# A two-layer decoder trunk on one core: norm sums of the heads by matmuls with ones, weights' low parts moved from GpSimd to VectorE, and a reordered start

## Chip, cores and metric

The kernel runs on one core of a Trainium2 chip. The metric is the device time of one execution in microseconds (us), median of the runs. The engines are TensorE (PE; its weight loads are listed as PEld), VectorE (DVE), ScalarE (ACT), GpSimd (POOL) and SyncE (SP), which issues most of the DMAs.

## What is computed

The input x has 512 tokens and 1024 features in float32. Layer 0 adds a causal pooling mixer and an MLP; then keys and values are projected once; layer 1 adds a differential attention of 8 heads over them and another MLP. The reference, cut:

```python
def _rmsnorm(x, g):
    y = x * lax.rsqrt(jnp.mean(x * x, axis=-1, keepdims=True) + EPS)
    return y * g

def _mlp(h, w_in, w_out):                 # 1024 -> 4096 -> 1024
    return jnp.square(jax.nn.relu(h @ w_in)) @ w_out

# layer 0: window means over 2, 4, 8, 16 tokens, one window for each of 4 groups of 256 features
m = pooled - hg                           # hg: _rmsnorm(x, norm_mix[0]) by groups
x = x + einsum('bsgc,gcd->bsgd', m, pool_w) * pool_scale
x = x + _mlp(_rmsnorm(x, norm_mlp[0]), w_mlp_in[0], w_mlp_out[0])
kv = _rmsnorm(x, kv_norm) @ w_kv
k = _rmsnorm(kv[..., :1024].reshape(b, s, 8, 2, 64), k_norm)
v = kv[..., 1024:].reshape(b, s, 8, 128)
# layer 1, for each head with its two key and query halves c
q = _rmsnorm((h @ w_q).reshape(b, s, 8, 2, 64), q_norm) * 64 ** -0.5
p = softmax(q_c @ k_c.T + bias[distance], causal)
o = (p[:, :, 0] - lam * p[:, :, 1]) @ v
x = x + _rmsnorm(o, subln) * (1 - lambda_init) @ w_o
x = x + _mlp(_rmsnorm(x, norm_mlp[1]), w_mlp_in[1], w_mlp_out[1])
```

## The kernel before

Features lie on the 128 partitions and tokens along the free axis (`xT`, 8 chunks of 128 x 512). Each large product is made of three matmuls (`product`, L1373): every operand is split into a high part (fp32r, rounded by ACT) and a low part (the rest, made by a subtraction), and high x high, high x low and low x high are summed in a PSUM bank. There are eight banks, `O[0:4]` and `I[0:4]`. Weights come through two raw buffers of 128 x 2048; ACT writes `w_high`, DVE `w_low` (`split_low`, L914). A unit counter runs through them: `w_high`, `w_low` and `w_used` count units split and used. Each engine has its own stream of instructions, written out by hand, and semaphores tie them together; the order in a stream is the order of execution.

**Start** (before L1542). x is loaded by token, its squares are summed on ACT (L719), and three tiles of 128 tokens are scaled on DVE (L1129) and one on ACT (L728), while PE turns x into `xT`. Then PE mixes: for each of 8 chunks one matmul by zeros over the whole bank (L1516), which opens the sum, and four matmuls of tokens with the bands (L1519). ACT and DVE split the result. After all eight mixes and a small bias product (L1526) come the 48 matmuls with the pooling weights (L1530), and then MLP 0. One weight unit in this stretch is split on Pool.

**MLPs** (`mlp`, L1469). Input units of 256 columns, then per quarter seven products of a Strassen-like scheme. The change doesn't touch them.

**Heads.** Unit `U_HEAD + 2n` holds the K and Q weights of head n (2 x 1024 columns of buffer 1), the next unit the V weights (buffer 0). During head h PE makes the scores of h and then projects K, Q, V of head n = h + 1 (`head`, L1633). K and Q must be normed over 64 features, which lie on partitions. So ACT copies the projection out of PSUM (`kf`, `qf`), PE turns it (`turn`, L1561: four transposes of 128 x 128), ACT squares what it turned (`square_raw`, L772), DVE reduces over 64 columns (`kq_reduce`, L1173) and adds eps, ACT takes the root, DVE inverts it and spreads it over the columns of `ksq` and `qsq` (`kq_inverses`, L1193), PE turns these back, and DVE multiplies (`kq_norms`). The output O of a head is normed the same way one head later (`of`, `o_squares`, `o_sums`, `o_inverses`, `o_norm`). The order on PE in a head is: scores of tiles 0 and 1, turns of V and O, scores of tiles 2 and 3, projection of K (24 matmuls), of Q (24), turn of the probabilities (10 transposes), turns of K and Q as projected, 18 matmuls of V's projection, turns of the spread K, Q and O norms, 6 matmuls of V, and probabilities by values. In head 0 there is no projection of K, as it is made earlier. The low parts of the K and Q weights are made on Pool in two halves (`split_low_halves`, L540), and DVE passes the news on (`pass_low`, L921). Heads 1 to 6 are one loop. Between MLP 0 and head 0 lies a passage: K, Q and V of head 0, the statistics of the norm before K and V (`norm_stats`, L1382, four matmuls of 128 x 128 with two columns of ones), and K of head 1. The last head is written apart and runs beside the output projection (`wo_part`).

## Time and profile before

| | us |
|---|---|
| median of 3 runs | 969.94 (968.29 to 970.57) |
| the profiled execution | 970.49 |
| its span on the core | 968.7 |

| engine | busy us | share | instructions |
|---|---|---|---|
| PE | 954.0 | 98% | 5143 |
| PEld | 813.1 | 84% | 5143 |
| DVE | 681.1 | 70% | 959 |
| ACT | 464.6 | 48% | 588 |
| POOL | 82.3 | 8% | 66 |

The chain of work that ended last is PE's for 85% of the span, DVE's for 7%, ACT's for 4%. Matmuls overlap with the next ones, so their durations don't add up; the distance from one start to the next does. A number behind `x` in the rows counts records. In brackets or behind the last bar stands the engine's idle time and what ended it.

### The profile page before, as it was taken

To read this page: it belongs to the slowest core of one execution; us is meant where nothing else is said; L and a number is where in the kernel's file an instruction comes from. 1 tells how busy PE (TensorE), PEld (TensorE's weight loads), DVE (VectorE), ACT (ScalarE), POOL (GpSimd) and SP (SyncE) were. 2 spreads that over 40 slices of the span, in tenths; PEclk is the share of its full clock that TensorE was granted. 3 is DMA by queue.
4 is the path that set the end of the run, shared out by engine and by line. 5 is a ranking of instruction groups with operands and counts; after the bars stand their busy time and mean duration, and the time that the engine had idled before them with its cause. 6 is when DMAs were issued, how large, how long until landed. Compare 5 with 4: busy or idle time off the path is not lost.

```text
span 968.7 us, 13034 instructions
## 1 busy us (share of the span) xinstructions
PE 954.0 (98%) x5143; PEld 813.1 (84%) x5143; DVE 681.1 (70%) x959; ACT 464.6 (48%) x588; POOL 82.3 (8%) x66
## 2 busy tenths in 40 slices
PE   8999999999999999999999999999999999999998
PEld 7788998998898898778888887888888888888877
DVE  4976766666676678877777777667767676677685
ACT  7644334334333437576666765345433433433432
POOL 1201000000000000122222220000000000010010
PEclk9999999999999999999999999999999999999999
DMA  6427682385457534143232222334676269238534
GB/s 228 138 84 232 131 260 87 88 228 163 118 113 205 160 59 130 44 115 86 72 86 84 78 74 93 109 102 113 191 200 191 90 125 261 89 87 225 165 98 120
DMA packets 99212, 128.94 MB, mean 133 GB/s; under 512 B 3201, under 2 KB 61618, under 8 KB 99162
## 3 DMA queue, kind: packets, MB, share of 16 engines
q1 hardware_dynamic: 85178, 98.33, 30.8%
q0 software_dynamic: 13984, 29.91, 16.8%
q8 instruction: 35, 0.57, 0.2%
q14 instruction: 15, 0.12, 0.0%
HBM read 126.11 MB, written 4.74 MB: 135 GB/s over the span
## 4 chain that ended last, share of the span: by engine, by line
PE 85%; DVE 7%; ACT 4%; issue 3%; DMA 1%; SPq 0%; DVEq 0%; ACTq 0%
PE bank L1375 27%; PE bank L1377 26%; PE bank L1376 26%; PE bank L1565 2%; DVE w_low L918 2%; PE bank L1575 2%; DVE kq_sum_buf L1175 1%; ACT w_high L655 1%; PE bank L1519 1%; DMA work<-in_x_dram 1%; ACT h_high_buf L613 1%; ACT w_high L607 0%; DVE work L1273 0%; ACT a_high_buf L812 0%; DVE a_low_buf L1244 0%
## 5 line engine op out<-in xcount | busy, mean ns | idle before, releaser
L1375 PE MATMUL bank<-h_high_buf,w_high 128*128 128x512 f32 x640 | 252.5, 394 | 0.7 <-DVE h_low_buf L927 0.4
L1377 PE MATMUL bank<-h_high_buf,w_low 128*128 128x512 f32 x640 | 249.4, 390 | 0.0
L1376 PE MATMUL bank<-h_low_buf,w_high 128*128 128x512 f32 x640 | 249.2, 389 | 0.0
L918 DVE TENSOR_TENSOR w_low<-raw,w_high 128x2048 fp32r<-128x2048 f32 (+1 forms) x68 | 147.3, 2166 | 66.8 <-ACT w_high L655 49.1
L1375 PE MATMUL bank<-a_high_buf,w_high 128*128 128x256 f32 (+1 forms) x592 | 184.4, 312 | 2.2 <-DVE a_low_buf L927 1.4
L1377 PE MATMUL bank<-a_high_buf,w_low 128*128 128x256 f32 (+1 forms) x592 | 183.0, 309 | 0.0
L1376 PE MATMUL bank<-a_low_buf,w_high 128*128 128x256 f32 (+1 forms) x592 | 182.8, 309 | 0.0
L1375 PEld LDWEIGHTS bank<-h_high_buf,w_high 128*128 128x128 f32 x640 | 120.2, 188 | 28.7 <-issue 2.2
L1377 PEld LDWEIGHTS bank<-h_high_buf,w_low 128*128 128x128 f32 x640 | 120.1, 188 | 25.4
L1376 PEld LDWEIGHTS bank<-h_low_buf,w_high 128*128 128x128 f32 x640 | 120.3, 188 | 23.6
L664 ACT ACTIVATE work<-work 128x512 f32<-128x512 f32 x64 | 40.1, 632 | 181.3 <-DVE work L971 181.2
L655 ACT ACTIVATE w_high<-raw 128x2048 fp32r<-128x2048 f32 x40 | 76.5, 1912 | 94.2 <-PE bank L1377 90.9
L1375 PEld LDWEIGHTS bank<-a_high_buf,w_high 128*128 128x128 f32 x592 | 113.0, 191 | 10.0 <-issue 2.3
L1377 PEld LDWEIGHTS bank<-a_high_buf,w_low 128*128 128x128 f32 x592 | 113.0, 191 | 5.8
L1376 PEld LDWEIGHTS bank<-a_low_buf,w_high 128*128 128x128 f32 x592 | 113.1, 191 | 5.4
L971 DVE SCALAR_TENSOR_TENSOR work<-bank,rstd_bc 128x512 f32<-128x512 f32 x64 | 43.5, 687 | 70.9 <-PE bank L1377 70.7
L1375 PE MATMUL bank<-w_high,a_high_buf 128*128 128x512 f32 x224 | 87.7, 392 | 1.5 <-DVE w_low L918 1.1
L1376 PE MATMUL bank<-w_low,a_high_buf 128*128 128x512 f32 x224 | 87.2, 389 | 0.0
L1377 PE MATMUL bank<-w_high,a_low_buf 128*128 128x512 f32 x224 | 87.2, 389 | 0.0
L987 DVE TENSOR_TENSOR a_low_buf<-work,a_high_buf 128x1792 fp32r<-128x1792 f32 (+2 forms) x34 | 64.9, 1909 | 6.1 <-ACT a_high_buf L671 6.1
L594 ACT ACTIVATE w_high<-raw 128x2048 fp32r<-128x2048 f32 (+1 forms) x29 | 48.5, 1673 | 33.1 <-PE bank L1377 33.1
L671 ACT ACTIVATE a_high_buf<-work 128x1792 fp32r<-128x1792 f32 (+2 forms) x34 | 54.5, 1602 | 7.4 <-DVE work L982 7.4
(152 smaller groups left out, 1171.1 us busy)
## 6 DMA issues: line engine op xcount, KB each, us to landing
raw<-in_w_mlp_out_dram SPq DMA_DIRECT2D x24, 1024.0 KB, 6.2
raw<-in_w_mlp_out_dram POOLq DMA_DIRECT2D x24, 1024.0 KB, 8.7
raw<-in_w_mlp_in_dram SPq DMA_DIRECT2D x16, 1024.0 KB, 5.5
work<-in_w_mlp_out_dram SPq DMA_DIRECT2D x8, 1024.0 KB, 4.7
work<-in_w_mlp_in_dram SPq DMA_DIRECT2D x8, 1024.0 KB, 6.7
raw<-in_w_kv_dram SPq DMA_DIRECT2D x16, 512.0 KB, 4.0
xT<-in_w_mlp_out_dram SPq DMA_DIRECT2D x8, 1024.0 KB, 4.7
xT<-in_w_mlp_in_dram SPq DMA_DIRECT2D x8, 1024.0 KB, 7.0
```

Of the source, the lines that this page charges most:

```text
L594: act.activation(w_high_buf[s][:, 0:cols], src[:, 0:cols], ACT.Copy).then_inc(w_high, 1)
L655: act.activation(w_high_buf[u % 2][:, :], mlp_raw[l][OUT_RAW[p]], ACT.Copy).then_inc(w_high, 1)
L664: act.activation(b[:, 0:8:7, :] if j == 0 else b[:, A12:A22 + 1, :], relu_buf[j].rearrange("p (h n) -> p h n", h=2), ACT.Square)\
L671: act.activation(operand(a_high_flat, n, first, last), pre[n % 2][:, first:last, :].rearrange("p s n -> p (s n)"), ACT.Copy)\
L918: dve.tensor_tensor(w_low_buf[s][:, 0:cols], src[:, 0:cols], f32(w_high_buf[s][:, 0:cols]), ALU.subtract)\
L971: dve.scalar_tensor_tensor(relu_buf[j], I[2 * (n % 2) + j][:, :], 0.0, rstd_bc, ALU.max, ALU.mult).then_inc(z_taken, 1)
L987: dve.tensor_tensor(operand(a_low_flat, n, first, last), pre[n % 2][:, first:last, :].rearrange("p s n -> p (s n)"), f32(operand(a_high_fl ...
L1375: pe.matmul(acc, w_hi, m_hi, start=start, stop=False, skip_group_check=onto)
L1376: pe.matmul(acc, w_hi, m_lo, start=False, stop=False, skip_group_check=onto)
L1377: return pe.matmul(acc, w_lo, m_hi, start=False, stop=stop, skip_group_check=onto)
L1565: last = pe.transpose(b[:, i * P:(i + 1) * P], src[:, i * P:(i + 1) * P], ident[:, :])
L1575: done = pe.matmul(O[b + c][:, 0:n], w[r, q], m[r, 0:n], start=first, stop=last)
```

## The change

For the heads:

- The squares of K, Q and O are taken on ACT from the bank of the projection itself. PE sums them over the partitions by four matmuls of 128 x 128 with two columns (`column_sums`), with `half_ones` (one for each half of 64 partitions) for K and Q, and with `all_ones` for O. The turns of K, Q and O as projected go, and so do the three reduces on DVE.
- K and Q are handled apart, each with semaphores of its own: K's sum stands in the middle of Q's projection, the turn of K's spread norm behind it, ahead of the turn of the probabilities.
- Pool subtracts nothing in the heads. DVE makes the low parts of the K and Q weights, the Q half behind the scores of tiles 0 and 1 (`kq_weights_rest`), the K half behind `k_low` (`kq_weights_first`).
- Head 6 is written out, as `head(H - 2, ..., last=True)`, and splits two parts of the output projection's input, which now lie at chunks 10 and 15.

For the start and the passage: the roots of all token tiles are taken together, tile 3 is squared on DVE, the bands are loaded behind the parameters, the matmuls by zeros go, the pooling weights are split in two halves, all on ACT and DVE, and the pooling products stand between the mixes. The dot products for lambda move behind the pooling. In the passage V's weights are split earlier, and the projections are interleaved in another order.

The diff, cut:

```diff
+        half_ones = sb("half_ones", [P, 2])
...
-            sp.dma_start(band_sb, bands).then_inc(bands_landed, 16)
...
+            sp.dma_start(band_sb, bands).then_inc(bands_landed, 16)
...
-                split_low_halves(h, POOL_UNITS[1 + h])
...
-            for i in range(TT):
+            for i in range(TT - 1):
                 act.wait_ge(x_landed[i], 16)
                 act.activation(h_tok[:, i, :], x_tok[:, i, :], ACT.Square, accum_out=tok_ss[:, i:i + 1]).then_inc(tok_sq, 1)
...
+            act.wait_ge(tok_last_sq, 1)
+            act.activation(tok_root[:, :], tok_ss[:, :], ACT.Sqrt, scale=1.0 / D, bias=eps[:, 0:1]).then_inc(tok_rooted, 1)
...
+            act.activation(w_high_buf[0][:, 0:UNIT // 2], raw[0][:, 0:UNIT // 2], ACT.Copy).then_inc(pool_half_high, 1)
...
+            def head(h, first, last=False):
+                n = h + 1
                 exps(h)
+                bring_table(ACT.Sqrt)
                 if not first:
-                    o_squares(h - 1, I[3])
-                copy_k(h + 1)
-                split_v(h + 1)
-                bring_table(ACT.Sqrt)
-                copy_q(h + 1)
-                split_high_first(U_HEAD + 4 + 2 * h, kq_landed(h + 2))
-                at_highs(h)
-                project(h + 1)
-                kq_roots(h + 1)
+                    square_k(n)
+                    copy_k(n)
+                split_v(n)
+                if last:
+                    o_high(0)
+                    o_high(1)
+                k_root(n)
+                split_high_first(n + 1, kq_landed(n + 1))
+                square_q(n)
+                copy_q(n)
+                k_high(n)
+                at_highs(h, range(1))
+                q_root(n)
                 if not first:
-                    o_roots(h - 1)
+                    o_roots(h - 1, I[3])
+                at_highs(h, range(1, 3))
                 bring_table(ACT.Exp)
-                kq_highs(h + 1)
-                split_high_rest()
+                q_high(n)
+                split_high_rest(U_HEAD + 2 + 2 * n)
                 o_copies(h, I[3])
+                o_squares(h, I[3])
...
+            dve.wait_ge(x_landed[TT - 1], 16)
+            dve.tensor_tensor_reduce(out=h_tok[:, TT - 1, :], in0=x_tok[:, TT - 1, :], in1=x_tok[:, TT - 1, :], scale=1.0, scalar=0.0,
+                                     op0=ALU.mult, op1=ALU.add, accum_out=tok_ss[:, TT - 1:TT]).then_inc(tok_last_sq, 1)
...
                 scores(h, 0)
                 scores(h, 1)
-                pass_low(h + 1)
+                kq_weights_rest(n)
                 combine(h, 0)
                 v_lows(h)
...
                 combine(h, 3)
-                split_low(U_HEAD + 3 + 2 * h, 0, 1024)
-                if not first:
-                    o_sums(h - 1)
-                at_lows(h)
-                kq_sums(h + 1)
-                kq_inverses(h + 1)
+                split_low(U_HEAD + 1 + 2 * n, 0, 1024)
+                if last:
+                    o_low(0)
+                    o_low(1)
+                add_k_eps(n, I[0])
+                k_inverses(n)
+                k_norm(n, I[0])
+                add_q_eps(n, I[1])
+                at_lows(h, range(1))
+                q_inverses(n)
                 if not first:
                     o_inverses(h - 1)
-                kq_norms(h + 1)
+                at_lows(h, range(1, 3))
+                k_low(n)
+                kq_weights_first(n + 1)
+                q_norm(n, I[1])
                 if not first:
                     o_norm(h - 1, O[3])
-                kq_lows(h + 1)
-                take_v(h + 1)
+                q_low(n)
+                take_v(n)
...
-                pe.matmul(I[c % 4][:, :], a_high_buf[:, 0, 0:P], a_high_buf[:, 0, :], start=True, stop=False)
...
+            for c in range(4):
+                mix(c)
+            pe.wait_ge(pool_half_low, 1)
+            pe.wait_ge(xt_copied, len(ACT_CHUNKS))
+            pool_group(0)
+            mix(4)
+            mix(5)
...
+            pool_group(1, lambda: pe.wait_ge(bias_rows_ready, 2))
+            mix(6)
+            mix(7)
+            pe.wait_ge(w_low, 1)
+            pool_group(2)
+            pool_group(3)
             mlp(0)
...
+            def column_sums(b, src, ones):
+                for i in range(TT):
+                    last = pe.matmul(b[:, 2 * i:2 * i + 2], src[:, i * P:(i + 1) * P], ones[:, :], start=True, stop=True)
+                return last
...
-                    turn(of, I[3], o_copied, h - 1, o_raw_turned)
+                    o_sums(h - 1, I[3])
...
-                project(None, 1, 1024, I[1], a_high_buf, a_low_buf, w_used)
+                project(None, 1, 1024, I[1], a_high_buf, a_low_buf, None, range(0, 4))
+                k_sums(n, I[0])
+                project(None, 1, 1024, I[1], a_high_buf, a_low_buf, w_used, range(4, KC))
+                turn(ksq, I[0], k_spread, n, k_turned)
                 turn_probs(h)
-                turn_raw(n)
+                q_sums(n, I[1])
                 pe.wait_ge(w_low, U_HEAD + 2 + 2 * n)
                 pe.wait_ge(v_low, n)
-                project(None, 0, 0, I[2], h_high_buf, h_low_buf, None, range(0, 6))
-                turn(ksq, I[0], k_spread, n, k_turned)
+                project(None, 0, 0, I[2], h_high_buf, h_low_buf, None, range(0, 5))
                 turn(qsq, I[1], q_spread, n, q_turned)
                 if not first:
                     turn(osq, O[3], o_spread, h - 1, o_turned)
-                project(None, 0, 0, I[2], h_high_buf, h_low_buf, w_used, range(6, KC))
+                project(None, 0, 0, I[2], h_high_buf, h_low_buf, w_used, range(5, KC))
```

## Rows read from the trace of the kernel before

**Rows 1.** The page: busy us, share of the span and instructions of each engine.

```profile
PE 954.0 (98%) x5143; PEld 813.1 (84%) x5143; DVE 681.1 (70%) x959; ACT 464.6 (48%) x588; POOL 82.3 (8%) x66
```

**Rows 2.** Stretches: length, then busy us by engine, PEclk, DMA share, GB/s.

```profile
0.00:24.90 24.90, 21.25 (x115) 18.06 (x116) 12.08 (x16) 18.67 (x30) 3.55 (x10) 0.93 0.70 232
...
374.64:402.65 28.01, 26.54 (x126) 20.42 (x124) 23.00 (x35) 18.82 (x31) 0.87 (x1) 1.00 0.20 57
402.65:424.43 21.78, 19.50 (x116) 15.64 (x116) 18.23 (x51) 15.72 (x34) 5.61 (x5) 1.00 0.35 100
424.43:577.44 153.01, 152.43 (x878) 126.07 (x877) 111.03 (x318) 103.33 (x222) 35.21 (x24) 1.00 0.30 86
```

**Rows 3.** Timeline of PE in head 2: start, us, engine, line, form, count.

```profile
450.82 1.09 PE L1565 MATMUL bank<-ident,work 128*128 128x128 f32 x8
...
465.39 1.04 PE L1565 MATMUL bank<-ident,work 128*128 128x128 f32 x8
...
470.63 1.54 PE L1565 MATMUL bank<-ident,work 128*128 128x128 f32 x12
```

**Rows 4.** Waits of PE's weight loads: us in total, times, longest.

```profile
PEld bank L1565 <- DVE work L1198: 4.2, 7, 1.1
```

**Rows 5.** Timeline of PE in MLP 0, around a norm sum and a turn.

```profile
50.15 0.95 PE L1390 MATMUL bank<-all_ones,work 128*128 128x2 f32 x8
50.96 0.49 PE L1375 MATMUL bank<-h_high_buf,w_high 128*128 128x512 f32 x1
51.28 0.40 PE L1376 MATMUL bank<-h_low_buf,w_high 128*128 128x512 f32 x1
...
54.51 0.60 PE L1396 MATMUL bank<-ident,work 128*128 128x128 f32 x4
54.86 0.48 PE L1375 MATMUL bank<-h_high_buf,w_high 128*128 128x512 f32 x1
```

**Rows 6.** Groups by line: count, busy us, mean ns, idle time before.

```profile
L1390 PE MATMUL bank<-all_ones,work 128*128 128x2 f32 x24 | 2.9, 245 | 0.4 <-DVE work L1273 0.4
```

**Rows 7.** Timelines of POOL, ACT and DVE in head 2.

```profile
448.99 2.38 POOL L548 TENSOR_TENSOR w_low<-raw,w_high 128x1024 fp32r<-128x1024 f32 x1 [5.96 <-ACT w_high L610]
...
459.55 1.05 ACT L594 ACTIVATE w_high<-raw 128x1024 fp32r<-128x1024 f32 x1
460.62 1.28 ACT L797 ACT_TABLE_LOAD   x1
...
460.63 1.23 DVE L918 TENSOR_TENSOR w_low<-raw,w_high 128x1024 fp32r<-128x1024 f32 x1 [1.08 <-ACT w_high L594]
```

**Rows 8.** Timeline of DVE in head 0.

```profile
404.11 0.28 DVE L1227 CUSTOM_DVE_ANT_0 work<-bank,work 128x128 f32<-128x128 f32 x1
...
412.86 1.22 DVE L918 TENSOR_TENSOR w_low<-raw,w_high 128x1024 fp32r<-128x1024 f32 x1
```

**Rows 9.** Timelines of ACT, DVE, PE and POOL at the start.

```profile
10.89 1.15 ACT L728 ACTIVATE work<-work,tok_rstd 128x1024 f32<-128x1024 f32 x1
...
12.04 2.05 ACT L732 ACTIVATE xT<-bank 128x512 f32<-128x512 f32 x4
...
14.79 0.75 DVE L927 SCALAR_TENSOR_TENSOR a_low_buf<-bank,params,a_high_buf 128x512 fp32r<-128x512 f32 x1 [1.49 <-ACT a_high_buf L613]
...
17.49 0.47 PE L1516 MATMUL bank<-a_high_buf 128*128 128x512 f32 x1
...
22.70 4.58 POOL L537 TENSOR_TENSOR w_low<-raw,w_high 128x2048 fp32r<-128x2048 f32 x1 [20.45 <-ACT w_high L594]
22.78 4.59 DVE L1143 CUSTOM_DVE_ANT_0 work<-work 128x64 f32<-128x64 f32 x1
...
36.25 0.39 PE L1375 MATMUL bank<-h_high_buf,w_high 128*128 128x512 f32 x1
```

**Rows 10.** A short stretch at the start, columns as in rows 2, and a DMA issue.

```profile
14.00:15.00 1.00, 1.00 (x6) 1.00 (x5) 0.21 (x1) 0.66 (x2) 0.00 (x0) 0.50 1.11 355
...
work<-in_bands_dram SPq DMA_DIRECT2D x1, 572.0 KB, 7.9
```

More of the change, by code:

```diff
@@ L531, in _ @@
             done(pool.memset(all_ones[:, :], 1.0))
+            done(pool.memset(half_ones[:, :], 0.0))
+            done(pool.memset(half_ones[0:HD, 0:1], 1.0))
+            done(pool.memset(half_ones[HD:P, 1:2], 1.0))
             pool.memset(eps[:, :], EPS).then_inc(consts_ready, 1)
@@ new lines, in _ @@
+            act.wait_ge(params_ready, 1)
+            mix_high(0)
+            mix_high(1)
+            copy_xt(0)
+            act.activation(w_high_buf[0][:, UNIT // 2:], raw[0][:, UNIT // 2:], ACT.Copy).then_inc(w_high, 1)
+            mix_high(2)
+            mix_high(3)
+            split_in(0, 0)
+            mix_high(4)
+            mix_high(5)
+            act.wait_ge(bias_done, 1)
+            act.activation(bias_rows[0:H, 0:S], O[3][0:H, :], ACT.Copy).then_inc(bias_rows_ready, 1)
+            mix_high(6)
@@ L843, in _ @@
-            square_raw(0, 1, qsq)
             norm_root_step(NORM_KV)
-            kq_roots(0)
+            k_root(0)
+            q_root(0)
             bring_table(ACT.Exp)
-            kq_highs(0)
-            split_high_rest()
-            def head(h, first):
+            act.wait_ge(lam_dot, 2)
+            act.activation(lam_exps[:, :], lam_dots[:, :], ACT.Exp).then_inc(lam_exp, 1)
+            k_high(0)
+            q_high(0)
+            split_high_rest(U_HEAD + 2)
+            square_k(1)
@@ new lines, in _ @@
+            mix_low(1)
+            dve.wait_ge(w_high, 1)
+            dve.tensor_tensor(w_low_buf[0][:, UNIT // 2:], raw[0][:, UNIT // 2:], f32(w_high_buf[0][:, UNIT // 2:]), ALU.subtract)\
+               .then_inc(w_low, 1)
+            mix_low(2)
+            mix_low(3)
+            dve.wait_ge(xt_copied, len(ACT_CHUNKS))
+            add_pooled(0)
+            add_pooled(1)
+            mix_low(4)
+            mix_low(5)
+            add_pooled(2)
+            add_pooled(3)
+            mix_low(6)
@@ L1284, in _, with head @@
             dve.wait_ge(kq_eps_ready, 1)
[L1285 to L1288 removed]
+            add_k_eps(0, O[0])
+            add_q_eps(0, O[1])
             norm_invert(NORM_KV)
+            k_inverses(0)
+            q_inverses(0)
             norm_keep(NORM_KV, I[3])
+            k_norm(0, O[0])
+            q_norm(0, O[1])
             take_v(0)
+            k_low(0)
+            q_low(0)
+            dve.wait_ge(lam_exp, 1)
+            dve.tensor_scalar(neg_lam[:, :], lam_exps[:, 1:2], lam_exps[:, 0:1], -LAMBDA_INIT, ALU.subtract, ALU.add).then_inc(lam_ready, 1)
             dve.wait_ge(lam_ready, 1)
[L1294 removed]
+            def head(h, first, last=False):
+                n = h + 1
                 dve.wait_ge(t_landed, 16 * h + 16)
@@ new lines, in _ @@
+            for c in range(4):
+                mix(c)
[4 more added lines that the diff above has]
+            mix(5)
+            pe.wait_ge(bias_in_landed, 32)
+            pe.wait_ge(x_ready, X_POOL)
+            pe.matmul(O[3][0:H, :], rel_sb[:, :], bucket_sb[0:NB, :], start=True, stop=True).then_inc(bias_done, 1)
+            pool_group(1, lambda: pe.wait_ge(bias_rows_ready, 2))
+            mix(6)
```

412 lines of the change are left out of this document (212 added, 200 removed).

## Prediction

> **What bounds the kernel now.** I read the page's busy shares first: the matmul engine (PE) is busy in 98% of the span, VectorE (DVE) 70%, ScalarE (ACT) 48% and GpSimd (Pool) 8% [rows 1]. A busy PE is not yet PE at its peak, so the second view is the table of stretches, which I cut where the code changes stage [rows 2]. It shows PE busy for 152.4 of 153.0 us in heads 1 to 6 (25.50 us a head). Only three stretches leave it idle: the start (3.7 of 24.9 us), the passage from MLP 0 to the first head (1.5 of 28.0), and head 0 (2.3 of 21.8). The third view is the timeline of PE alone, where distances from start to start give the true price of an instruction, since ends overlap. In the steady head the only wait worth a name is that of the twelve turns at 470.63 for the spread K norms [rows 3], 4.2 us over seven heads as the waits view has it, in part hidden by the pipeline [rows 4]. So in the heads an instruction taken off DVE or Pool gains nothing, and each put on PE costs its full time.
>
> **Turns replaced by sums (24 times).** Before, the norm of K, Q and O of each head goes: a turn (4 transposes on PE), a square on ACT, a reduce on DVE. After, ACT squares the projection as it is, and PE sums over its partitions by 4 matmuls with ones, 2 columns wide. PE loses one turn and gains one sum, for each of K, Q, O in 8 heads. The kernel already does both things elsewhere. A turn starts at 54.51 and the product after it at 54.86: 0.35 us. A sum of the same form (128x128 stationary f32, 2 columns moving) starts at 50.15 and the next product at 50.96: 0.81 us; its row says x8, two records for each of the 4 matmuls [rows 5], and the groups by line have 24 records for 12 such matmuls [rows 6], while the two turns at 450.82 are x8, one record for each transpose [rows 3]. A swap therefore costs 0.81 - 0.35 = 0.46 us of PE. Among other turns I take the same difference: 4 records of 0.11 more. 24 swaps are 11.0 us, if PE has no slack to put them in.
> The Trainium skill's page "TensorE: Matmul & The Clock Gate" (section Back-to-back issue gap) gives matmuls of 1 to 64 columns a floor near 25 ns. By that rule, an estimate from this page, a sum would take 0.1 us and each swap would gain 0.25. The trace disagrees: 0.81 us for such a sum [rows 5]. The rule is a rival below.
>
> **The steady head.** Before, a head has a chain of 18 transposes (10 of L1601 for the probabilities, then L1565 x8 at 465.39), one of 12 (470.63) and one of 8 inside the scores (450.82) [rows 3]. After: scores hold turn V and the O sum (+0.46); K's sum stands alone inside the Q projection (+0.81, and 0.09 for one more break in the run of products, as 0.32 against 0.23 shows behind a sum [rows 5]); the turn of the spread K, the turn of the probabilities and the Q sum follow each other (14 turns and 8 sum records against 18 turns, +0.46); then turns of Q and O (8 instead of 12, -0.45). That is +1.37. The wait for the spread norms goes, since K's are now made during the Q projection: -0.31. I sum 25.50 + 1.06 = 26.56 us.
> Is that cover real? I laid ACT and DVE against it, from the start of the head's scores. DVE takes over the low parts of the K and Q weights, twice 1024 columns. DVE's own row for 1024 columns is 1.23 us, next to 2.38 on Pool [rows 7]: +2.3 us in all, and its three reduces go. The first half stands behind the first scores, on DVE's queue in front of combine and the later scores; it ends at +2.9, PE wants it at +3.8. DVE ends its last combine at 0.6 + 8.75 [rows 8] + 1.15 = +10.5. ACT ends its exponentials near +8.8, then come a table load (1.3), square and copy of K (0.5 each) and V's high part (1.05) until +12.3 [rows 7], and V's low part on DVE until +13.5. K's root, inverse and spread end at +14.5, while PE comes to the turn at +15.8: 1.3 us to spare. The Q sum needs the copy of Q at +17.0, PE is there at +17.3. The normed O of the head before must be ready at +24.7, and is at +24.4, as the other half of the weights (1.15) stands before it. ACT's square of O ends at +1.2, PE wants it at +1.3. Four margins, two of them thin. Covered, they cost nothing; uncovered, about 0.5 us a head. Heads 1 to 6: 6 x 1.06 = +6.4. Head 6 also has two O parts split on DVE and ACT ahead of K's sum: +0.4.
>
> **Head 0** has no K projection (it is made earlier), so it lacks those 5.5 us of cover. DVE's chain from the first scores (404.11) to V's low part (412.86) takes 8.75 [rows 8] without a break, and ACT's exponentials end before its last combine does. After, with scores at 403.4 and 1.15 more in it, the last combine ends at 413.3; ACT brings the square-root table (1.3) and splits V (1.05) until 414.1; DVE's low part ends at 415.25 and K's spread at 416.3. PE, done with the Q projection and K's sum at 412.2, now has the turn of the spread K ahead of the probabilities and waits about 4.2 us, where before it waited 2.3 in the whole head. Walked on, scores of head 1 start at 426.7 against 424.43 [rows 2].
>
> **Passage to the first head.** Two sums (+0.9), a wait of 1.0 for V's low weights and 0.7 for the inputs of the Q projection are new; the waits for kv sums, for the turned norm and for V mostly go, as V is scaled earlier. My walk gives scores of head 0 at 402.8 against 402.65, so +0.15, between -1.5 and +1.5 (the idle time there is 1.5 [rows 2]). With head 0: +2.3.
>
> **Last head and output projection.** One more sum (+0.46) inside the scores; but the probabilities' end no longer waits for the reduce of O on DVE: -0.85. Net -0.4.
>
> **The start.** The 8 matmuls by zeros go (each lies 0.31 ahead of what follows it, as the one at 17.49 does [rows 9]: 2.5 us), and pooling products move between the mixes. All tokens' roots are now taken together: the first scaling on DVE comes at 10.8 instead of 9.4. ACT scales tile 3 (1.15) and copies a bank before it copies the parameters, so the first mix goes from 12.3 to about 13.2. Then ACT has three bank copies (2.05 for 4) and half the pool weights (1.0) until 15.6, DVE its half (1.15) and two low parts (0.75 each, 0.66 from start to start) until 18.1 [rows 9]. From there PE has all its work: 48 products of 0.228 (10.95), 4 mixes of 0.87, the bias matmul 0.95 and breaks 0.2 make 15.6, so MLP 0 starts at 33.8 instead of 36.25 [rows 9]: -2.45. The granted clock fell to 0.50 from 14 to 15 us, the lower of its levels (1.2 GHz), after PE had waited for the parameters from about 10.9 to 12.3 [rows 10]; the same may come at another place, hence +-2. The bands are issued behind seven small parameter loads on SP's queue; they are 572 KB, took 7.9 us from issue among the loads of x [rows 10], and PE needs them only at 13.2, later than before; the loads ahead of them are 25 KB, so this is covered.
> The first custom instruction of DVE is an open price. It took 4.59 us for 64 columns at 22.78, beside a Pool subtraction from 22.70 of 4.58 [rows 9]. Both end together, so I hold it for blocked by Pool, and the new one (the square of tile 3) then costs about 1.2 at 9.0, when Pool does nothing. The Trainium skill, page "SBUF — State Buffer", section "SBUF: two separate sides", says the same: DVE with two SBUF inputs and GpSimd exclude each other for a whole instruction.
>
> **The sum** against the profiled execution, 970.49 us around a span of 968.7: -2.45 + 2.3 + 6.4 + 0.4 - 0.4 = +6.2, so 976.7. On the median of the runs, 969.94, it gives 976.1. The MLPs have the same code.
>
> **Rivals.** (1) Other side: a narrow sum is cheaper than a turn among other work. Place: the 24 sums; price: if its 8 records hid under running products down to 0.1 us, each swap would gain 0.25 instead of costing 0.46: 969.94 + 6.2 - 24 x 0.71 = 959.1. The kernel is faster than before once a swap comes out 0.26 us cheaper than I have it. For it: 2 columns instead of 128. Against it: [rows 5], measured between such products. Chance 7%. (2) The first custom instruction is slow of itself: DVE, ACT and PE start 3.5 to 4 us later; 980. For it: the first custom instruction of the program was the one of 4.59 [rows 9]. 10%. (3) DVE or ACT becomes late in each head, at one of the thin margins: 0.5 us x 7 = 3.5, 979.6. 13%. (4) The change doesn't bring head 0 and the passage the waits that I see: -4, 972.1. 10%. My forecast, 976.1 with 974 to 978 around it: 60%.
>
> **Range and chances.** 971.5 to 981 holds cases 2, 3, 4 and the forecast, with the clock's +-2 on the start; outside lies case 1 and some of a sum of 2 and 3. A measurement of this kernel can tell 0.2% (1.9 us) from no change. Faster 0.07 (case 1), within 0.06 (the low end of case 4), slower 0.87.
>
> **What would show it.** In the profile after: sums x8 with 0.8 us to the next product; steady heads of 26.5 us; PE waiting about 4 us at the first turn of K in head 0; MLP 0 starting near 33.8; the first custom instruction near 9 us lasting 1.2. A head shorter than 25.5 would break the first step, one above 27 the cover.

## The result and the profile after

The changed kernel takes 981.14 us, the median of its runs (980.11 to 983.11), beside 969.95 (968.29 to 970.57) for the kernel before: a ratio of 1.0119, interval 1.0103 to 1.0134, so 1.2% slower. The forecast was 976.1 with a range of 971.5 to 981.0. The direction was right; the time lies 5 us above the forecast and just above the range. The profiled execution is the 983.11 one, with a span of 981.3.

The page after, its rows of busy time and of PE's clock in 40 slices of 24.5 us:

```profile
PE 965.2 (98%) x5231; PEld 828.6 (84%) x5231; DVE 682.7 (70%) x961; ACT 461.4 (47%) x592; POOL 46.5 (5%) x54
...
PEclk8999999999999999989999999999999999999999
```

PE has 88 more records and 11.2 us more busy time than in [rows 1]; Pool has lost 36 us and DVE gained only 1.6, as the three reduces per head are gone. The new thing is in the PEclk row: an 8 in the first slice and an 8 in the eighteenth (417 to 441.6 us), behind the wait in head 0. The stretches of the code's stages say what each digit is worth. Columns as in [rows 2]: length, busy time by engine, PEclk, DMA share, GB/s; the stretches are the start until the first pooling product, the pooling, the passage, head 0, and heads 1 to 6.

```profile
0.00:20.46 20.46, 15.28 (x73) 13.56 (x74) 8.57 (x14) 12.79 (x21) 1.65 (x12) 0.83 0.72 245
20.46:36.44 15.98, 15.98 (x86) 13.08 (x84) 11.77 (x18) 8.77 (x13) 6.92 (x5) 1.00 0.46 129
374.98:403.34 28.36, 27.16 (x135) 21.38 (x134) 22.98 (x38) 20.13 (x35) 0.00 (x0) 1.00 0.20 56
403.34:431.63 28.29, 24.33 (x125) 20.28 (x124) 18.19 (x50) 16.11 (x35) 1.15 (x2) 0.82 0.29 77
431.63:590.60 158.97, 158.83 (x951) 135.50 (x950) 116.77 (x320) 104.50 (x230) 5.89 (x11) 1.00 0.29 83
```

Beside [rows 2] that gives a ledger. It is made from span to span (968.70 and 981.32), from one PE start to the next, and its lines add up to the difference of 12.62. In the last column the side after is taken from a run in which TensorE's clock stayed at 2.4 GHz in that stretch (the start from the one below with K's norm first, head 0 from the one with idle products); the side before is its profile as it is.

| stretch | before | after | change | forecast | at full clock |
|---|---|---|---|---|---|
| start to MLP 0 | 36.25 | 36.44 | +0.19 | -2.45 | -2.26 |
| MLP 0 to the passage | 338.39 | 338.54 | +0.15 | 0 | +0.15 |
| passage | 28.01 | 28.36 | +0.35 | +0.15 | +0.35 |
| head 0 | 21.78 | 28.29 | +6.51 | +2.15 | +2.31 |
| heads 1 to 6 | 153.01 | 158.97 | +5.96 | +6.8 | +5.96 |
| last head to the end | 391.27 | 390.72 | -0.55 | -0.4 | -0.55 |
| sum | 968.70 | 981.32 | +12.6 | +6.2 | +6.0 |

The start needs care, because the kernel before has a low clock there too, around the row of [rows 10]:

```profile
13.00:14.00 1.00, 1.00 (x9) 0.91 (x8) 0.30 (x1) 1.00 (x4) 0.00 (x0) 0.78 1.10 360
...
15.00:16.00 1.00, 1.00 (x6) 1.00 (x6) 0.54 (x1) 0.00 (x0) 0.00 (x0) 0.50 0.96 209
16.00:17.00 1.00, 1.00 (x6) 0.90 (x5) 0.20 (x1) 0.92 (x2) 0.00 (x0) 0.51 0.18 40
```

It is low from about 13.6 to 17.0 us, with PE busy all the time. In the two larger groups of runs of the kernel before, those with a mean clock of 0.998, as in its profile, have a median of 970.2, those with 1.0 one of 968.7. So an estimate of its start at full clock is 36.25 - 1.5 = 34.8. The changed start ends at 33.99 and 34.47 in the two profiles that have a whole clock there. Clock against equal clock the new order then brings 0.3 to 0.8 us and not 2.26, and the change as a whole costs 7.4 to 7.9 us and not 6.0. Where both sides have the clock low for 3.4 us the new order brings 1.2 to 1.5 (four profiles, 34.73 to 35.09).

**The heads.** The timeline of PE in head 1 of the kernel after (start, duration, line, form, records) answers to [rows 3]:

```profile
443.59 0.95 PE L1655 MATMUL bank<-half_ones,work 128*128 128x2 f32 x8
444.40 0.49 PE L1456 MATMUL bank<-a_high_buf,w_high 128*128 128x512 f32 x1
...
447.27 0.60 PE L1680 MATMUL bank<-ident,work 128*128 128x128 f32 x4
447.70 1.25 PE L1716 MATMUL bank<-ident,work 128*128 128x128 f32 x10
448.80 0.95 PE L1655 MATMUL bank<-half_ones,work 128*128 128x2 f32 x8
```

A sum has its 8 records and 0.81 us until the next product. Almost no idle time stands in these heads: 158.83 busy us in 158.97. So the steady head (1 to 5), 26.44 us, is the price of PE's instructions and nothing else. Head 6, with the two O parts, is 26.75.

**The start.** Timeline of PE, with idle time and its releaser in brackets, then the one custom instruction of DVE at the start, then the clock in short stretches:

```profile
9.38 1.09 PE L1581 MATMUL bank<-ident,work 128*128 128x128 f32 x8 [0.26 <-DMA work<-in_x_dram]
13.07 0.31 PE L1585 MATMUL bank<-ident,work 51*128 51x51 f32 x1 [2.60 <-ACT xT L732]
13.73 6.51 PE L1603 MATMUL bank<-work 128*128 128x143 f32 x28 [0.35 <-ACT params L743]
```

```profile
9.36 1.22 DVE L1171 CUSTOM_DVE_ANT_0 work<-work 128x1024 f32<-128x1024 f32 x1 [8.36 <-DMA work<-in_x_dram]
```

```profile
12.00:13.00 1.00, 0.00 (x0) 0.00 (x0) 1.00 (x2) 0.93 (x2) 0.00 (x0) 0.95 1.01 320
13.00:14.00 1.00, 0.58 (x2) 0.48 (x3) 1.00 (x3) 0.58 (x2) 0.00 (x0) 0.50 0.94 301
14.00:16.00 2.00, 2.00 (x10) 2.00 (x10) 1.11 (x2) 2.00 (x4) 0.00 (x0) 0.50 1.06 341
...
19.00:20.00 1.00, 1.00 (x7) 1.00 (x7) 0.32 (x2) 1.00 (x3) 0.00 (x0) 0.64 0.00 0
```

PE idles for 2.6 us before the turn of the parameters, the clock drops to its lower level (1.2 GHz) at the end of that, and the mixes then run on it: 28 matmuls of 143 columns take 6.5 us. The custom instruction takes 1.22 us for 1024 columns, not the 4.59 for 64 of [rows 9].

**Head 0.** PE's row at the turn of the spread K, and the clock around it:

```profile
417.02 1.11 PE L1680 MATMUL bank<-ident,work 128*128 128x128 f32 x4 [3.79 <-DVE work L1253]
```

```profile
413.00:417.00 4.00, 0.23 (x2) 0.00 (x0) 2.87 (x6) 2.62 (x5) 0.00 (x0) 0.83 0.49 135
417.00:419.00 2.00, 1.98 (x10) 1.98 (x11) 0.69 (x1) 1.29 (x4) 0.00 (x0) 0.50 0.83 237
...
423.00:425.00 2.00, 2.00 (x6) 1.56 (x5) 2.00 (x5) 1.47 (x2) 0.00 (x0) 0.50 0.00 0
425.00:426.00 1.00, 1.00 (x4) 0.76 (x4) 0.80 (x1) 0.00 (x0) 0.00 (x0) 0.55 0.00 0
```

The wait that was forecast (4.2 us) is there, 3.79 us for the spread norm made at L1253. What follows it is not in the forecast: from 417 to about 425.9 PE is busy at half clock. 8.9 us at half speed do what 4.45 would do at full speed. The run with idle products below has 4.2. The Trainium skill, page "TensorE: Matmul & The Clock Gate", section Terms, prices the penalty as the time below full clock times the share of pulses left out. By it, as an estimate, the whole low stretch, from about 415.7 to 425.9, would cost 5.1 us; that is more than the 4.2, as PE was idle until 417.0.

### The profile page after: what moved, and what is told of

Read it like the earlier page. It is cut to its first block, busy times and chain, and to the rows that moved or that the text cites. A ratio compares the mean times of both kernels' runs of the same rounds, so it can differ in the third digit from the quotient of the medians.

```text
span 981.3 us, 13176 instructions
## 1 busy us (share of the span) xinstructions
PE 965.2 (98%) x5231; PEld 828.6 (84%) x5231; DVE 682.7 (70%) x961; ACT 461.4 (47%) x592; POOL 46.5 (5%) x54
## 4 chain that ended last, share of the span: by engine, by line
PE 89%; DVE 5%; ACT 3%; issue 2%; DMA 1%; SPq 0%; DVEq 0%; ACTq 0%
PE bank L1456 28%; PE bank L1458 27%; PE bank L1457 27%; DVE w_low L952 2%; PE bank L1655 2%; PE bank L1680 2%; PE bank L1690 2%; PE bank L1603 1%; PE bank L1716 1%; ACT w_high L663 1%; DMA work<-in_x_dram 1%; ACT work L773 0%; ACT w_high L600 0%; ACT a_high_buf L621 0%; DVE work L1017 0%
## 5 line engine op out<-in xcount | busy, mean ns | idle before, releaser
L952 DVE TENSOR_TENSOR w_low<-raw,w_high 128x2048 fp32r<-128x2048 f32 (+1 forms) x67 | 145.0, 2164 | 69.7 <-ACT w_high L663 48.9
```

The lines of the kernel that those rows point to most:

```text
L952: dve.tensor_tensor(w_low_buf[s][:, 0:cols], src[:, 0:cols], f32(w_high_buf[s][:, 0:cols]), ALU.subtract)\
```

## The experiments

The theory that the ledger gives: the change costs (A) the sums, 8 records each on a PE that has no slack, (B) a wait in head 0 for K's norm, and (C) the clock that falls after PE's waits, at the start and in head 0. The rivals are that something else holds the start and head 0 (ACT's and DVE's splits), and that DVE, with the weights' low parts taken over from Pool, is late in each head. Each run stands beside runs of the kernel before on the same chip, with medians of 969.9 to 970.0 us in all three groups; the changed kernel itself has only its own four runs, so differences from its 981.14 are differences between groups. Unless something else is said, a kernel is the changed one with the edit shown.

### Idle products in head 0

```diff
+                if first:
+                    for _ in range(17):
+                        pe.matmul(I[3][:, :], h_high_buf[:, 0, 0:P], h_high_buf[:, 0, :], start=True, stop=True)
                 turn(ksq, I[0], k_spread, n, k_turned)
```

> The changed kernel with 17 matmuls of 128x512 without use put on PE in head 0, just ahead of the turn of K's spread norm, where PE waited 3.9 us. Theory A (what I missed is TensorE's clock: after this wait PE ran 8.6 us at 1.2 GHz, 417.0 to 425.6, which costs 4.3 us): the turn still starts near 417, the granted clock stays at 1.00 through head 0, head 0 falls from 28.3 to about 24.0 us and the time to about 977. Theory B (the slow stretch has another cause, such as a transfer or VectorE, and only shows as a lower clock): head 0 stays at 28.3 and the time at 981.

977.47 us, ratio 1.0082 (1.0066 to 1.0099). Timeline of PE and the clock around head 0's wait:

```profile
411.31 4.01 PE L1760 MATMUL bank<-h_high_buf 128*128 128x512 f32 x17
...
415.28 0.66 PE L1680 MATMUL bank<-ident,work 128*128 128x128 f32 x4
```

```profile
412.00:417.00 5.00, 5.00 (x31) 4.16 (x30) 2.86 (x6) 3.38 (x7) 0.00 (x0) 1.00 0.48 157
417.00:421.00 4.00, 4.00 (x24) 3.41 (x23) 3.11 (x8) 3.27 (x7) 0.00 (x0) 1.00 0.13 37
```

Work that computes nothing, put into the wait, makes the kernel 3.7 us faster. Head 0 takes 24.09 in place of 28.29, the clock is whole, and the turn of the spread K still comes when DVE is ready. So 4.2 us of head 0 were clock, and the wait itself with its consequences is 24.09 - 21.78 = 2.3.

### The probabilities turned first in head 0

```diff
+                if first:
+                    turn_probs(h)
                 turn(ksq, I[0], k_spread, n, k_turned)
-                turn_probs(h)
+                if not first:
+                    turn_probs(h)
```

> The changed kernel with one order on PE exchanged in head 0 alone: the turn of the probabilities (10 transposes) ahead of the turn of K's spread norm. Theory A (wait plus clock): the probabilities are ready near 413.5, so 1.1 us of work moves into the wait, which is cut in two of 1 and 2 us; if the clock stays up after these, head 0 is 28.3 - 1.1 - 4.3 = 22.9 us and the time 975.7; if it still falls, 27.2 us and 980. Theory B: 27.2 us and 980.

979.71 us, 1.0102 (1.0085 to 1.0119); its runs, 979.03 to 980.67, overlap those of the changed kernel. Head 0 is 26.71. The ten turns lie in the wait, which is then 2.33 us, with another of 0.65 for the copy of Q. The clock fell all the same:

```profile
412.00:416.00 4.00, 1.52 (x13) 1.05 (x12) 2.59 (x5) 2.62 (x6) 0.00 (x0) 1.00 0.34 123
416.00:418.00 2.00, 1.35 (x9) 1.14 (x7) 0.69 (x1) 1.75 (x4) 0.00 (x0) 0.56 0.88 256
418.00:422.00 4.00, 4.00 (x12) 3.33 (x13) 3.08 (x8) 2.69 (x6) 0.00 (x0) 0.50 0.02 5
```

Shortening the wait by the ten turns is worth less than filling it.

### Pool makes the low parts in the heads again

The second half of the K and Q weights and half of the next ones are subtracted on Pool, as in the kernel before; DVE only passes the news on.

```diff
+                if h:
+                    pool.wait_ge(half_high, n)
+                    pool.tensor_tensor(w_low_buf[1][:, 0:UNIT // 2], raw[1][:, 0:UNIT // 2], ...).then_inc(half_low, 1)
+                pool.wait_ge(half_low, n)
+                pool.wait_ge(w_high, U_HEAD + 2 * n + 1)
+                pool.tensor_tensor(w_low_buf[1][:, UNIT // 2:], raw[1][:, UNIT // 2:], ...).then_inc(pool_low, 1)
...
-                dve.wait_ge(w_high, U_HEAD + 2 * n + 1)
-                dve.tensor_tensor(w_low_buf[1][:, UNIT // 2:], raw[1][:, UNIT // 2:], ..., ALU.subtract).then_inc(w_low, 1)
+                dve.wait_ge(pool_low, n + 1)
+                dve.memset(pass_cell[:, :], 0.0).then_inc(w_low, 1)
...
-                kq_weights_first(n + 1)
```

> The changed kernel with Pool making the low parts of the K and Q weights again, as before (VectorE is spared 2 x 1.15 us a head), all else as changed. Theory A (PE is the bound in the heads, VectorE has cover there but not in head 0): steady heads stay at 26.44 us within 0.1; in head 0 the spread of K comes 1.15 us earlier, the wait of PE falls from 3.9 to 2.8 us, head 0 from 28.3 to 27.1, and less if the clock stays up after the shorter wait; time 980, or 976 with the clock up. Theory C (VectorE's added work is what costs in the heads): steady heads come near 25.5 us and the time near 974.

977.25 us, 1.0073 (1.0056 to 1.009). Two results in one. The steady heads, 1 to 5, are 26.44, to the hundredth those of the changed kernel: DVE's 2.3 us more per head are covered, and the rival that DVE is late in each head falls. Head 6 is 26.45, where the changed kernel has 26.75: there DVE is late by 0.3 us, and only there. In head 0, which has no projection of K to cover it, the transfer from Pool to DVE does cost:

```profile
415.62 1.12 PE L1687 MATMUL bank<-ident,work 128*128 128x128 f32 x4 [3.05 <-DVE work L1261]
```

The wait is 3.05 in place of 3.79, and the clock was low only from about 415.4 to 418.8; head 0 is 24.60. Head 0 gives 3.7 us of the difference between the two profiles; how much of it is a low clock that happened to be short, one profile can't say, but the medians differ by 3.9 too.

### K's sum made twice

```diff
-                column_sums(b, ksq, half_ones).then_inc(k_summed, 1)
+                column_sums(b, ksq, half_ones)
+                column_sums(b, ksq, half_ones).then_inc(k_summed, 1)
```

> The changed kernel with the sum for K made twice in each head (8 more sums of 4 matmuls). Theory A (each sum costs its full 0.81 us, 8 records at 0.112, as nothing hides it): steady heads go from 26.44 to 27.25 us, and all to 981.1 + 7 x 0.81 + less in head 0, where PE waits anyway = 986.8. Rival (narrow matmuls are cheap, most hides under the products): below 26.7 us a head, time 981 to 983.

985.60 us, 1.0162 (1.0144 to 1.018). PE in the head where K's sum is doubled:

```profile
441.54 1.84 PE L1655 MATMUL bank<-half_ones,work 128*128 128x2 f32 x16
443.24 0.49 PE L1456 MATMUL bank<-a_high_buf,w_high 128*128 128x512 f32 x1
```

1.70 us for two sums, and heads of 27.33: +0.89 each, a little over the 0.81 expected, at 0.11 for each of 8 records (head 6, which had the wait for DVE, gains 0.58). A sum hides behind nothing in the steady heads. This run showed something else besides. Its head 0 has a wait as well, but the clock stayed up there (24.06 us); it fell instead in the passage, from about 393.6 to 400.5:

```profile
380.00:390.00 10.00, 9.52 (x44) 7.51 (x43) 7.95 (x10) 8.45 (x16) 0.00 (x0) 1.00 0.05 14
390.00:400.00 10.00, 10.00 (x49) 8.70 (x49) 4.78 (x12) 3.20 (x8) 0.00 (x0) 0.68 0.01 2
```

PE's longest waits ahead of it in the passage, 0.72 and 0.48 us, are those of the changed kernel, where the clock stayed up, and the last of them ended 8 us before the fall. Why it fell there stays open.

### Sums on fp32r operands

ACT writes the squares rounded to fp32r, and the ones are fp32r.

```diff
+        half_r = sb("half_r", [P, 2], F32R)
+        all_r = sb("all_r", [P, 2], F32R)
+        ksr, qsr = w_high_buf[0][:, 1024:1536], w_high_buf[0][:, 1536:2048]
...
-                act.activation(ksq, I[0][:, :], ACT.Square).then_inc(kq_sq, 1)
+                act.activation(ksr, I[0][:, :], ACT.Square).then_inc(kq_sq, 1)
...
-                column_sums(b, ksq, half_ones).then_inc(k_summed, 1)
+                column_sums(b, ksr, half_r).then_inc(k_summed, 1)
```

> Changed part of the computation: the squares of K, Q and O are rounded to fp32r on ACT, and the ones are fp32r too, so the 24 norm sums of the heads run on fp32r operands. All else as in the changed kernel. Theory A (a sum costs 0.81 us because each of its 4 f32 matmuls runs as 2 records of 0.1 us): 4 records in place of 8, a sum 0.36 us, so each head with three sums is 1.35 us shorter, 25.1 in place of 26.44, the kernel 24 x 0.45 = 10.8 shorter, 981.1 - 10.8 = 970.3. Theory B (a sum costs its time through the change of stationary operand and the break in the run of products, whatever the type): heads stay at 26.3 to 26.44, 979 to 981. The wait in head 0 and its clock fall stay under both.

971.48 us, 1.0018 (1.0007 to 1.0028). The sums have 4 records now:

```profile
443.85 0.58 PE L1662 MATMUL bank<-half_r,w_high 128*128 128x2 f32 x4
444.29 0.48 PE L1463 MATMUL bank<-h_high_buf,w_high 128*128 128x512 f32 x1
...
464.30 0.50 PE L1662 MATMUL bank<-half_r,w_high 128*128 128x2 f32 x4
464.66 0.47 PE L1463 MATMUL bank<-a_high_buf,w_high 128*128 128x512 f32 x1
```

0.36 us from the sum at 464.30 to its product, where it was 0.81, and heads of 25.12. Theory A gave 25.1 and 970.3. The missing microsecond stands in head 6, 26.38 in place of 26.75, which gains only 0.37:

```profile
569.20 0.66 PE L1687 MATMUL bank<-ident,work 128*128 128x128 f32 x4 [1.03 <-DVE work L1260]
```

There the cover is used up: DVE splits two O parts (1.41 us) ahead of K's norm, and PE, faster now, waits 1.03 for it. So the price of the sums goes with their records, and with 4 a swap of a turn for a sum costs nothing (0.36 against 0.35 [rows 5]). Each record has a weight load of its own, in the PEld rows 8 for a sum on f32 and 4 on fp32r; the edit halves both, so whether the loads or the matmuls set the 0.1 us isn't separated. A head is then 0.38 us shorter than before, 25.12 against 25.50, which is close to the 0.31 that I had for the wait of [rows 4].

### Another order at the start

```diff
+            act.wait_ge(xt_done, TT)
+            copy_xt(4)
             act.wait_ge(tok_sq, TT)
...
+            act.wait_ge(params_turned, 1)
+            act.activation(params[:, :], I[0][:, 0:N_PARAM], ACT.Copy).then_inc(params_ready, 1)
...
             pe.wait_ge(params_ready, 1)
+            for _ in range(4):
+                pe.matmul(I[0][:, :], a_high_buf[:, 0, 0:P], a_high_buf[:, 0, :], start=True, stop=True)
+            pe.wait_ge(bands_landed, 16)
```

> Changed: ACT copies the bank of chunk 4 and the parameters before the root of the token sums and before it scales tile 3, and PE runs 4 idle products of 128x512 (results overwritten) while it waits for its first mix. Theory A (the changed start doesn't bring its 2.5 us because PE idles from 10.4 to 13.1 us and its clock is then 1.2 GHz until 19.5): no record below full clock up to 25 us, first pooling products by 18.5 and MLP 0 from about 33.8 to 34.2 in place of 36.44, kernel 2.3 shorter, 978.8. Theory B (the start is held by ACT and DVE, which split the mixes, not by the clock): MLP 0 at 36 or later, 981.

979.43 us, 1.0106 (1.0089 to 1.0123). PE at the start:

```profile
10.60 0.23 PE L1586 MATMUL bank<-ident,work 51*128 51x51 f32 x1 [0.78 <-ACT xT L729]
11.14 1.20 PE L1590 MATMUL bank<-a_high_buf 128*128 128x512 f32 x4 [0.30 <-ACT params L737]
12.18 0.70 PE L1606 MATMUL bank<-work 128*128 128x143 f32 x4
13.03 3.60 PE L1606 MATMUL bank<-work 128*128 128x143 f32 x28 [0.15 <-DVE work L1178]
...
17.50 0.47 PE L1457 MATMUL bank<-a_high_buf,w_high 128*128 128x512 f32 x1 [0.88 <-DVE a_low_buf L1186]
```

28 matmuls of the mixes take 3.60 us, where 28 took 6.51; the first pooling product starts at 17.50 and MLP 0 at 33.48. The kernel gains 1.7 of the 2.3 expected. One reason is that MLP 0's start in the changed kernel is not always the 36.44 of its profile. The start is the same code in eight profiles (the changed kernel's and those of seven edits that leave it alone, but for two copies of 2 columns in those with fp32r sums), and MLP 0 starts in them at 33.99, 34.47, 34.73, 34.85, 34.94, 35.09, 36.08 and 36.44. The clock is low there for none to 6.8 us, and the turn of the parameters, which waits for x, starts at 12.19 to 13.07. From that turn to MLP 0 it is 21.8 us in the two profiles with a whole clock, 22.1 in the four with 3.4 us of low clock, and 23.4 and 23.5 in the two with 6.8. So the clock costs 0.3 or 1.6 us of the start. With the other order it is 33.35 to 34.29 in five profiles, none of which shows a low clock between 10 and 20 us.

### K's norm ahead of V's weights in head 0

```diff
+                if first:
+                    k_root(n)
                 split_v(n)
...
-                k_root(n)
+                if not first:
+                    k_root(n)
...
+                if first:
+                    add_k_eps(n, I[0])
+                    k_inverses(n)
                 split_low(U_HEAD + 1 + 2 * n, 0, 1024)
...
-                add_k_eps(n, I[0])
-                k_inverses(n)
+                if not first:
+                    add_k_eps(n, I[0])
+                    k_inverses(n)
```

> The changed kernel with one change of order, in head 0 alone: DVE's sum with eps, inverse and spread of K's norm stand ahead of the low part of V's weights (1.15 us and 0.75 of waiting for its high part), and ACT's root of K ahead of that high part. Theory A (PE's wait of 3.95 us in head 0 is the queue of V's weights on ACT and DVE in front of K's norm): the turn of the spread K comes 1.9 us earlier, the wait is about 2.0, the clock stays up or falls for shorter, head 0 is 22.5 to 24.5 in place of 28.3, the kernel 975.5 to 979. Theory B (the exponentials and combines hold it, V's weights do not): wait stays near 3.9 and head 0 near 28.

975.83 us, 1.0078 (1.0055 to 1.0101): the best single edit of those that keep the sums, with three calls moved in one head of eight. Its median is 5.3 us under the changed kernel's. Timeline of PE:

```profile
412.59 0.66 PE L1687 MATMUL bank<-ident,work 128*128 128x128 f32 x4 [1.83 <-DVE work L1256]
413.08 1.25 PE L1723 MATMUL bank<-ident,work 128*128 128x128 f32 x10
414.85 1.02 PE L1662 MATMUL bank<-half_ones,work 128*128 128x2 f32 x8 [0.51 <-ACT work L783]
```

The wait goes from 3.79 to 1.83, and the clock stays whole in this profile, with head 0 at 22.86. Beside the 24.09 of the run with idle products, whose clock in head 0 is whole too, the order itself is worth 1.2 us; the rest of the 5.3 I put down to clock that didn't fall, at the start included, where the edit changes nothing. It isn't safe from the fall: the mean clocks of its four runs are 1.0, 0.998, 1.0 and 0.993, and the last of them took 979.17. So V's weights, 1.15 us on DVE and the high part on ACT in front of them, were what K's norm stood behind. This profile also had a whole clock at the start, and so shows the start as forecast: PE again waits 2.41 us at the turn of the parameters, yet

```profile
10.00:13.00 3.00, 0.46 (x3) 0.39 (x4) 2.83 (x6) 2.28 (x5) 0.00 (x0) 1.00 1.09 367
13.00:16.00 3.00, 3.00 (x27) 3.00 (x27) 2.04 (x4) 3.00 (x6) 0.00 (x0) 1.00 1.03 311
```

and MLP 0 starts at 33.99 (forecast 33.8). With the clock whole, DVE holds the start:

```profile
17.99 0.47 PE L1463 MATMUL bank<-a_high_buf,w_high 128*128 128x512 f32 x1 [1.16 <-DVE a_low_buf L1188]
```

PE has done its four mixes and waits 1.16 us for the low part of one. That is the rival of the start, and it is true there; the forecast had it as well, with DVE's parts done at 18.1.

### Remedies together

Two kernels have fp32r sums and the 17 idle products of head 0; the second has the other order of the start besides.

> Both remedies of the heads: squares and ones of the norm sums as fp32r, and 17 idle products of 128x512 in head 0 ahead of the turn of the spread K norm. If the two costs are apart (theory A): 977.5 - 10.8 = 966.7, head 0 at 23.7, steady heads at 25.1, so faster than the kernel before by 0.3%. If theory B of the sums holds: 976.5 to 977.5.

968.62 us, 0.999 (0.998 to 1.0): head 0 at 23.64, steady heads at 25.13. The costs add up as separate ones; the 1.9 us over the 966.7 expected are sums that don't give their full 0.45. Beside the profile with idle products alone, head 6 gives 0.37 for its three sums, head 0 gives 0.45 for two and the passage 0.5 for two, together 1.8 short. The low clock explains little of it, as the two runs with a mean clock of 1.0 took 968.03 and 968.36.

> As the kernel with fp32r sums and idle products in head 0, with the reordered start (ACT copies the parameters early, 4 idle products before the first mix) besides. Theory A: 966.7 less up to 1.7 us, as MLP 0 starts at 33.8 to 34.2 in place of 34.7 to 36.4: 965 to 966. Theory B of the start: no difference to the one without it.

967.73 us, 0.9982 (0.9973 to 0.9992), above the 965 to 966 expected by about as much as the run before it was above its own: MLP 0 at 33.35. Three more put fp32r sums and the other start together with another head 0. In the first, the probabilities are turned first and 12 idle products follow:

```diff
                 if first:
                     turn_probs(h)
+                    for _ in range(12):
+                        pe.matmul(I[3][:, :], h_high_buf[:, 0, 0:P], h_high_buf[:, 0, :], start=True, stop=True)
                 turn(ksq, I[0], k_spread, n, k_turned)
```

> fp32r sums, reordered start, and in head 0 the turn of the probabilities ahead of the turn of the spread K, with 12 idle products of 128x512 between them. The turn of the probabilities then hides in the wait: head 0 about 22.6 in place of 23.65, MLP 0 at 33.4, steady heads 25.12, kernel 966.7 in place of 967.7.

967.51 us, 0.998 (0.9971 to 0.999). Head 0 is 23.42, not 22.6: of the turn of the probabilities only 0.2 us were hidden, because its last four wait 0.59 us for DVE's last combine, and the Q sum then waits 0.44 for ACT. The second has no idle products in head 0 and K's norm ahead of V's weights:

> fp32r sums, reordered start, probabilities' turn first in head 0, no idle products there, and K's norm ahead of V's weights in head 0 on ACT and DVE. The turn of the spread K can then start about when the probabilities are turned, so PE waits under 1 us there and again some 0.5 us for V's low weights; the clock doesn't fall. Head 0 at 21.5 to 22.3, kernel 966. If V's low weights become the wait instead, head 0 is 23 to 23.6 and the kernel 967.5.

968.05 us, 0.9988 (0.9978 to 0.9998). Its profile has head 0 at 22.38 and a span of 964.8, shorter than the 966.2 of the one above, but its runs spread from 966.35 to 969.82, with mean clocks of 0.996 to 1.0. Its waits in head 0 are 0.61, 0.36 and, for the square and copy of Q on ACT, 1.60 us. The third is the same with 4 idle products behind the turn of the probabilities:

> As the one with K's norm ahead of V's weights, with 4 idle products (0.9 us) after the turn of the probabilities. If waits of 1 us still cost clock: faster than without them. If not: the same or up to 0.5 us slower.

966.49 us, 0.9968 (0.9957 to 0.998), the fastest of all, 0.3% faster than the kernel before. Head 0 as in the kernel without the 4 idle products:

```profile
411.17 1.17 PE L1778 MATMUL bank<-h_high_buf 128*128 128x512 f32 x4
412.17 0.60 PE L1697 MATMUL bank<-ident,work 128*128 128x128 f32 x4
414.03 0.58 PE L1672 MATMUL bank<-half_r,w_high 128*128 128x2 f32 x4 [1.26 <-ACT work L791]
```

Four idle products make head 0 no shorter in the profile (22.39 against 22.38). What they change is the spread, with runs from 966.28 to 967.11 and mean clocks of 0.998 to 1.0, and so the median by 1.6 us. In the kernel without them the time goes with the mean clock: its two runs at 1.0 took 966.35 and 966.57, the five at 0.998 967.62 to 968.55, the three at 0.996 968.89 to 969.82. With them one run of seven is under 1.0. That they work through the clock is argued from these figures; no profile of a disturbed run of either kernel was taken, so the place of the low clock isn't shown.

## Why the prediction was right and where it was wrong

**The swaps and the steady head: right.** The sum as measured in MLP 0 [rows 5] is the sum as it costs in a head, 0.81; a steady head is 26.44 where I had 26.56, heads 1 to 6 +5.96 for +6.8. The doubled sum and the fp32r sums show that the price goes with the 8 records (and their weight loads) and not with the break. Rival 1 (narrow sums cheap) is refuted. The Trainium skill, page "TensorE: Matmul & The Clock Gate", section Back-to-back issue gap, gives 1 to 64 columns an issue floor near 25 ns, for a matmul taken by itself, and says that at small widths this leaves out the weight loads. The runs have 0.11 us for each of the 8 records, and 0.36 for a sum of 4 records on fp32r.

**The cover on DVE: right.** Heads 1 to 5 are the same with Pool's help and without. Rival 3 is refuted. The cover is thin, as I had it: head 6 loses 0.3 us to it (26.75 for 26.45 with Pool; forecast 0.4), and with shorter sums 1.0.

**The custom instruction: right.** 1.22 us at 9.36, with Pool doing nothing, and the one of 64 columns, which the change moves behind the pooling, is short now:

```profile
41.30 0.21 DVE L1232 CUSTOM_DVE_ANT_0 work<-work 128x64 f32<-128x64 f32 x1
```

So the 4.59 of [rows 9] was the time of Pool's subtraction. Rival 2 is refuted.

**Passage and last head: near.** +0.35 for +0.15, -0.55 for -0.4.

**The start: a right walk, and two terms that were mis-sized.** With the clock whole MLP 0 starts at 33.99 or 34.47 for 33.8. But I entered the clock as "+-2" around zero, when the change makes PE's idle stretch longer: 2.4 to 2.6 us at the turn of the parameters. The kernel before waited there for 1.01 us and then for 0.94, from 10.1 and not from 10.9 as I had it, and its clock fell at 13.6, when PE had been busy again for 1.3 us. And I set a walk at full clock against a start that itself had the clock low for 3.4 us: about 1.5 of my -2.45 is that, by the estimate above, and not the 8 matmuls by zeros. The profile had +0.19, 2.6 more than forecast: 1.6 of it is clock, the rest a first mix at 13.73 for 13.2 and 16.0 us from the first pooling product to MLP 0 where I had 15.7. Over the eight profiles MLP 0 starts on average at 35.07, 1.3 later than forecast.

**Head 0: the wait was right, its consequence was missing.** The walk gave a wait of 4.2 us and +2.15 for head 0; the chip gave 3.79 and, at full clock, +2.31. The step that failed is the one that stopped at the wait. I had read at the start that the clock falls to its lower level after PE has waited, and didn't apply it to the longest new wait of the change, so its cost stood in the sum as nothing. In the profile it is 4.2 us (28.29 against 24.09), the largest error of the sum. Rival 4, that this wait doesn't come, is refuted.

**The sum.** With the side after at full clock the ledger is +6.0 against +6.2, and as close as that by luck: the start is compared with one that has a low clock, and at full clock on both sides it is +7.4 to +7.9. The clock adds 1.6 at the start and 4.2 in head 0 in the profiled execution; the median of the runs, 981.14 against 983.11, has some 2 us less of it. The range took in +-2 of clock in one place, and had none in the other; with 4 us for head 0 its upper end would have held the result. One reading was wrong without harm: PE has idle time behind head 6 as well, 6.1 us from 577.4 to the end, not in three stretches only.

## What to carry to other kernels

Where a change makes the matmul engine wait for some microseconds, price the wait twice: once for itself, and once for a stretch at half clock that may follow. Here the second price was 4.2 us behind a wait of 3.79, 0.3 or 1.6 at the start behind one of 2.60, and nothing in other profiles with such waits. See also whether the kernel that you compare with pays it in the same stretch. Then look first at what stands in the queues of the other engines ahead of the one small result that it waits for, and only then at filling the wait with idle products. A matmul on f32 operands has twice the records of one on fp32r; where the moving side was 2 columns wide, that doubling was all that a sum cost more than a turn (0.81 and 0.36 us against 0.35).

## What the runs showed that I had not expected

- The clock is a matter of chance at waits of this size. After the same 2.60 us of idle PE at the start it stayed up in one profile, was low for 3.4 us in four and for 6.8 in two; in head 0 it fell in four of five profiles with one wait of 2.89 to 4.26 us, for 3 us in one and for 8.9 in another. The fifth, with the shortest of these waits, had it fall in the passage before, in a stretch where PE was busy. The kernel before pays for it too, in most of its runs. So one profile doesn't price a clock term; several, or the spread of the runs, do.
- Idle matmuls, 17 of 0.23 us, made a kernel 3.7 us faster, and with 4 of them in place of a wait of 0.36 us the spread of the runs was 0.8 us, without them 3.5.
- A small order change in one head out of eight (K's norm ahead of 1.15 us of weights) lowered the median by 5.3 us, of which 1.2 are the order itself; the rest I put down to the clock.
